# Gate weights kept in HBM tile by tile instead of column chunk by column chunk

## The reference

```
s = einsum('thpd,hpnd->thpn', q, sub_keys)              # 8 heads, 2 halves, 128 keys each
top_s, top_i = top_k(s, 16);  cand = sums of all pairs
best_s, best_c = top_k(cand, 16)                        # 16 experts per head and token
ids = i1 * 128 + i2;  gates = softmax(best_s)           # 128 experts per token
a = einsum('tkd,td->tk', expert_down[ids], x)
act = gelu(a) * gates
y = einsum('tk,tkd->td', act, expert_up[ids])
```

## Time and profile before

| | |
|---|---|
| median of 3 runs | 1579.66 us (1577.53 to 1579.83) |
| profiled execution | 1579.83 us, of which the span is 1578.0 us |
| mean granted TensorE clock | 0.987 of full speed |
| TensorE busy | 94% of the span |
| VectorE, ScalarE, GpSimd busy | 76%, 40%, 37% |
| HBM read, written | 360.49 MB, 42.99 MB |

### The profile page before, as it was taken

One profiled execution on the slowest core, in us unless ns is written; L12 is line 12 of the kernel. 1 busy time (PEld: TensorE's weight loads), 2 busy tenths in 40 slices (PEclk: granted clock), 3 DMA queues, 4 the chain that ended last, 5 costly groups with the idle time before them and its releaser, 6 DMA issues.

```text
span 1578.0 us, 21497 instructions
## 1 busy us (share of the span) xinstructions
PE 1487.3 (94%) x7670; PEld 1279.7 (81%) x7670; DVE 1199.6 (76%) x2406; ACT 623.7 (40%) x984; POOL 583.8 (37%) x459
## 2 busy tenths in 40 slices
PE   3999997999999889999978999999999999999997
PEld 3575545998888779999977888888888888888886
DVE  6546435678999987888836788787787888888887
ACT  1114333343434446666633333333333333333333
POOL 0000011225455436898821333343333443444340
PEclk9999998999999999999989999999999999999999
DMA  9962300446544436678678998999999999999983
GB/s 332 358 236 107 107 27 14 137 154 215 172 160 150 132 117 215 236 288 288 245 281 309 346 358 323 358 342 339 355 308 367 334 342 368 356 332 370 349 310 124
DMA packets 167945, 404.89 MB, mean 257 GB/s; under 512 B 20824, under 2 KB 83872, under 8 KB 166816
## 3 DMA queue, kind: packets, MB, share of 16 engines
q1 hardware_dynamic: 129152, 243.87, 44.2%
q0 software_dynamic: 36864, 134.23, 23.8%
q10 hardware_dynamic: 1824, 25.43, 4.0%
HBM read 360.49 MB, written 42.99 MB: 256 GB/s over the span
## 4 chain that ended last, share of the span: by engine, by line
PE 62%; DVE 12%; issue 4%; POOL 2%; DMA 2%; ACT 2%; SPq 0%; DVEq 0%; POOLq 0%; ACTq 0%
PE bank L1703 11%; PE bank L1704 10%; PE bank L1705 10%; PE bank L1647 8%; PE bank L1649 8%; PE bank L1648 8%; PE bank L1685 4%; DVE dlo L1209 2%; DVE cand L1253 2%; POOL gated L678 2%; DMA down<-in_down_t 1%; DVE topi L1199 1%; DVE top L1196 1%; PE bank L1592 1%; PE bank L1591 1%
## 5 line engine op out<-in xcount | busy, mean ns | idle before, releaser
L1647 PE MATMUL bank<-h2hi,dhi 128*128 128x384 f32 x1024 | 351.4, 343 | 38.2 <-DVE dlo L1209 36.8
L1649 PE MATMUL bank<-h2hi,dlo 128*128 128x384 f32 x1024 | 346.0, 338 | 0.0
L1648 PE MATMUL bank<-h2lo,dhi 128*128 128x384 f32 x1024 | 345.8, 338 | 0.0
L1209 DVE TENSOR_TENSOR dlo<-down,dhi 128x1024 fp32r<-128x1024 f32 x128 | 168.0, 1313 | 179.5 <-ACT dhi L826 179.4
L1703 PE MATMUL bank<-uhi,ahi 128*128 128x512 f32 x768 | 300.1, 391 | 3.5 <-DVE ulo L1381 3.5
L1704 PE MATMUL bank<-ulo,ahi 128*128 128x512 f32 x768 | 300.0, 391 | 0.0
L1705 PE MATMUL bank<-uhi,alo 128*128 128x512 f32 x768 | 299.6, 390 | 0.0
L645 POOL DMA_INDIRECT rows<-in_peer_down,ids x128 | 156.0, 1219 | 259.6 <-DVE rows L1222 221.1
L645 POOL DMA_INDIRECT rows<-in_peer_up,ids x128 | 159.5, 1246 | 246.2 <-DVE y L1231 221.9
L1647 PEld LDWEIGHTS bank<-h2hi,dhi 128*128 128x128 f32 x1024 | 194.7, 190 | 47.2 <-DVE dlo L1209 43.0
L1648 PEld LDWEIGHTS bank<-h2lo,dhi 128*128 128x128 f32 x1024 | 195.0, 190 | 2.7
(11 more groups left out here) (198 smaller groups left out, 2019.7 us busy)
## 6 DMA issues: line engine op xcount, KB each, us to landing
down<-in_down_t SPq DMA_DIRECT2D x128, 512.0 KB, 5.5
up<-in_peer_up SPq DMA_DIRECT2D x128, 512.0 KB, 6.6
ada<-in_w_ada SPq DMA_DIRECT2D x12, 2048.0 KB, 16.3
gate<-gates_dram SPq DMA_DIRECT2D x32, 768.0 KB, 10.4
gates_dram<-stage ACTq DMA_DIRECT2D x5, 4096.0 KB, 13.6
gel_dram<-gel SPq DMA_DIRECT2D x80, 192.0 KB, 2.1
gelu<-gel_dram SPq DMA_DIRECT2D x80, 192.0 KB, 5.8
wq<-in_peer_query SPq DMA_DIRECT2D x16, 512.0 KB, 4.7
```

The lines of the kernel that those rows point to most:

```text
L1209: ve.tensor_tensor(dlo[s][:], down[s][:], dhi[s][:].bitcast(F32), ALU.subtract).then_inc(dve_dlo, 1)
L1647: pe.matmul(bank[7 * s][:, 0:TD], dhi[s][:, k, :], h2hi[:, k, 0:TD], start=k == 0, stop=False)
L1648: pe.matmul(bank[7 * s][:, 0:TD], dhi[s][:, k, :], h2lo[:, k, 0:TD], start=False, stop=False)
L1649: last = pe.matmul(bank[7 * s][:, 0:TD], dlo[s][:, k, :], h2hi[:, k, 0:TD], start=False, stop=k == KT - 1)
```

## The change

The HBM tensor that holds the gates between the two stretches gets another order of axes. Before it is `[chunk, p, tile, 64 tokens]`; after it is `[tile, p, 384 tokens]`. So:

- A store still moves the same bytes of the same `stage` buffer, 4 MB per full chunk. Before, a partition's 32 KB land in one piece. After, they land as 128 pieces of 64 tokens (256 bytes), one in each tile's block, and with all partitions that makes 16384 pieces per chunk.
- A load fetches one tile (192 KB, 1536 bytes per partition) instead of four (768 KB, in pieces of 1 KB). 128 loads replace 32, in three buffers `gate0` to `gate2` instead of two for each of two groups. Each load waits for the product that last read its buffer.
- VectorE's product reads its gates as one plain row of 384 instead of six pieces of 64.
- The freed room changes places: one of the two late `rows` buffers moves from the second `stage` buffer's room to the first one's, so that its first gather waits for fewer stores. SyncE's wait for the second part of the last store moves to the first up step that needs it, and the last early tile's steps are written in another order.

```diff
-        gate = [[r(f"gate{g}_0", [CHUNKS, GSET, CHUNK_T])] for g in range(2)]
+        gate = [r(f"gate{i}", [TD]) for i in range(SLOTS)]
+        gelu = [r(f"gelu{i}", [TD]) for i in range(SLOTS)]
+        rows += [r(f"rows{ROWS - 2}", [D])]
...
-        gates_dram = nc.dram_tensor("gates_dram", [CHUNKS, KEYS, TILES, CHUNK_T], F32).ap()
+        gates_dram = nc.dram_tensor("gates_dram", [TILES, KEYS, TD], F32).ap()
...
-            def load_gates(n):
-                g, k = int(n >= EARLY), n % EARLY // GSET
-                sp.dma_start(gate[g][k % 2][:], gates_dram[:, :, n:n + GSET, :].rearrange("w p i t -> p w i t")
-                             ).then_inc(gate_in[g][k % 2], 16)
+            def load_gate(u):
+                if u >= SLOTS:
+                    sp.wait_ge(dve_act, u - SLOTS + 1)
+                sp.dma_start(gate[u % SLOTS][:], one(gates_dram, UPS[u])).then_inc(gate_in[u % SLOTS], 16)
...
             early(EARLY - 2)
-            next_down(EARLY - 1, 1)
             sp.wait_ge(stored[1], 16 * (CHUNKS // 2 - 1))
             sp.wait_ge(stored_part[0], 32)
-            for n in (0, EARLY):
-                load_gates(n)
-            store_gel(EARLY - 1, 1)
+            for u in range(SLOTS):
+                load_gate(u)
+            early(EARLY - 1)
             next_down(EARLY, 0)
...
+                        sp.wait_ge(stored_part[1], 32)
                         for s in range(2):
                             sp.wait_ge(gel_out[s], 16 * (EARLY // 2))
+                    load_gate(u)
                     load_gel(u)
                     load_up(u)
-                    for first in range(0, TILES, GSET):
-                        if first % EARLY and max(UP_AT[first - 2], SLOTS) == u:
-                            sp.wait_ge(stored_part[1], 32)
-                            if first % EARLY >= 2 * GSET:
-                                sp.wait_ge(dve_act, UP_AT[first - GSET - 1] + 1)
-                            load_gates(first)
...
             for n in range(asked, ROW_OPS):
-                if n == DOTS_EARLY + ROWS_KEPT:
+                if n == DOTS_EARLY + ROWS_KEPT + ROWS_ROUNDS - 1:
...
             def store_chunk(w, keys_1, signal):
-                act.dma_start(gates_dram[w, :, keys_1, :], stage[w % 2][:, keys_1, :]).then_inc(signal, 16)
+                act.dma_start(gates_dram[keys_1, :, w * CHUNK_T:(w + 1) * CHUNK_T].rearrange("i p t -> p i t"),
+                              stage[w % 2][:, keys_1, :]).then_inc(signal, 16)
...
-                ve.tensor_tensor(gelu[j][:].rearrange("p (w t) -> p w t", w=CHUNKS),
-                                 got[:].rearrange("p (w t) -> p w t", w=CHUNKS),
-                                 gate[g][k % 2][:, :, UPS[u] % GSET, :], ALU.mult).then_inc(dve_act, 1)
+                ve.wait_ge(gate_in[j], 16 * (u // SLOTS + 1))
+                ve.tensor_tensor(gelu[j][:], got[:], gate[j][:], ALU.mult).then_inc(dve_act, 1)
```

More of the change, by code:

```diff
@@ L116 @@
 assert sorted(UPS) == list(range(TILES))
-GSET = 4
-assert EARLY % GSET == 0 and TILES % GSET == 0 and 2 * GSET <= 16
 AHEAD = 2
@@ L343, in build_block @@
         alo = [r(f"alo{i}", [TD], F32R) for i in range(SLOTS)]
-        gelu = [r(f"gelu{i}", [TD]) for i in range(2)]
         r = Region(nc, stage_at, stage_at + KEYS * CHUNK_T * 4)
@@ L347, in build_block @@
         ulo += [r(f"ulo{i}", [D], F32R) for i in range(1, SLOTS)]
-        gelu += [r("gelu2", [TD])]
-        gate = [[r(f"gate{g}_0", [CHUNKS, GSET, CHUNK_T])] for g in range(2)]
+        gate = [r(f"gate{i}", [TD]) for i in range(SLOTS)]
+        gelu = [r(f"gelu{i}", [TD]) for i in range(SLOTS)]
+        rows += [r(f"rows{ROWS - 2}", [D])]
         r = Region(nc, stage_at + KEYS * CHUNK_T * 4, stage_at + 2 * KEYS * CHUNK_T * 4)
-        for g in range(2):
-            gate[g].append(r(f"gate{g}_1", [CHUNKS, GSET, CHUNK_T]))
-        rows += [r(f"rows{i}", [D]) for i in range(ROWS_KEPT + ROWS_HEADS, ROWS)]
+        rows += [r(f"rows{ROWS - 1}", [D])]
         yn = [r(f"yn{i}", [D]) for i in range(2)]
@@ L391, in build_block @@
         up_in = [sem(f"up_in{i}") for i in range(SLOTS)]
-        gate_in = [[sem(f"gate_in{g}_{i}") for i in range(2)] for g in range(2)]
+        gate_in = [sem(f"gate_in{i}") for i in range(SLOTS)]
         gel_in = [sem(f"gel_in{i}") for i in range(SLOTS)]
@@ L554, in _ @@
             sp.wait_ge(stored[0], 16 * (CHUNKS // 2))
-            sp.wait_ge(act_g, TD // 4)
             for u in range(SLOTS):
@@ L558, in _, with in_part0 @@
             early(EARLY - 2)
-            next_down(EARLY - 1, 1)
             sp.wait_ge(stored[1], 16 * (CHUNKS // 2 - 1))
             sp.wait_ge(stored_part[0], 32)
-            for n in (0, EARLY):
-                load_gates(n)
-            store_gel(EARLY - 1, 1)
+            for u in range(SLOTS):
+                load_gate(u)
+            early(EARLY - 1)
             next_down(EARLY, 0)
-            assert all(n < AFTER_G or n >= EARLY for n in UPS[:SLOTS])
+            def in_part0(n):
+                return n < 16 or EARLY <= n < EARLY + 16
+            whole_u = next(u for u, n in enumerate(UPS) if not in_part0(n))
+            assert all(n < AFTER_G or n >= EARLY for n in UPS[:whole_u])
             u = SLOTS
@@ L573, in _ @@
                 elif u < TILES:
-                    if u == SLOTS:
+                    if u == whole_u:
+                        sp.wait_ge(stored_part[1], 32)
                         for s in range(2):
                             sp.wait_ge(gel_out[s], 16 * (EARLY // 2))
+                    load_gate(u)
                     load_gel(u)
                     load_up(u)
-                    for first in range(0, TILES, GSET):
-                        if first % EARLY and max(UP_AT[first - 2], SLOTS) == u:
-                            sp.wait_ge(stored_part[1], 32)
-                            if first % EARLY >= 2 * GSET:
-                                sp.wait_ge(dve_act, UP_AT[first - GSET - 1] + 1)
-                            load_gates(first)
                     u += 1
@@ L1369, in activations @@
                         ve.wait_ge(dve_alo, u - SLOTS + 1)
-                g, k = int(UPS[u] >= EARLY), UPS[u] % EARLY // GSET
-                ve.wait_ge(gate_in[g][k % 2], 16 * (k // 2 + 1))
-                ve.tensor_tensor(gelu[j][:].rearrange("p (w t) -> p w t", w=CHUNKS),
-                                 got[:].rearrange("p (w t) -> p w t", w=CHUNKS),
-                                 gate[g][k % 2][:, :, UPS[u] % GSET, :], ALU.mult).then_inc(dve_act, 1)
+                ve.wait_ge(gate_in[j], 16 * (u // SLOTS + 1))
+                ve.tensor_tensor(gelu[j][:], got[:], gate[j][:], ALU.mult).then_inc(dve_act, 1)
             def parts_lo(u):
```

## The result

The changed kernel takes 1589.13 us (median of seven runs, 1583.71 to 1594.43), the kernel before on the same occasion 1577.53 us (seven, 1576.98 to 1581.32). The ratio is 1.0054 with a 95% interval of 1.0034 to 1.0076: slower by half a per cent. Forecast were 1695 us in a range of 1605 to 1790. The profiled execution took 1590.72 us, 10.9 more than the profiled one of before.

The account below looks back on a forecast made before the run. TensorE was taken to bound the kernel, with store issues holding ScalarE and so stopping it. 107.5 + 6.7 + 4.1 - 2.7 = +115.6 us on 1579.8 gave 1695.4 us, range 1605 to 1790.

Parts of the forecast that it names:

- What bounds the kernel: Whole span: TensorE is busy for 94%; cheaper VectorE or DMA work in the plan stretch is worth nothing.
- A chunk has 1025: ScalarE stands for 875 of them: Store issues of full chunks: entries per engine beyond about 150 hold ScalarE 22.4 us; five chunks cost +107.5 us.
- The 150 entries of the prediction: DMA queue: about 150 entries per engine can wait, worked out from SyncE's long issues at the trace's start.
- A piece of 256 bytes: Gate stores: each small write takes 25.6 ns per engine, the length of one read record.
- Rival 1: Gate stores: each small write costs double, 37.6 ns, giving 1758 us; chance 0.20 for 1740 to 1800.
- From a hold to TensorE's delay: Gates stretch: a 26.6 us hold, less cover, plus slow clock, costs TensorE 21.5 us per full chunk.
- B - 7.4 + 2.3: Cost per full chunk: B is hold plus other traffic, 26.6 us; 7.4 is TensorE's cover, 2.3 the slow clock.
- The last chunk: Last store, four parts: ScalarE free after 24 us, TensorE going on at 825.1 against 818.36 before.
- +6.7, +4.1 and -2.7: Last chunk: TensorE goes on later, +6.7 us; one down tile further back, +4.1; smaller first gate load, -2.7.
- Rival 3: Stores: the issue doesn't hold ScalarE and down loads slip between small pieces; 1567 us, chance 0.10, of which 0.06 faster.
- the cheap end of the failed step: Store hold: the queue takes more or a piece is cheap; 1618 us at 11 ns, chance 0.12 for 1600 to 1640.
- the three signs given for being wrong: Store issues under 7 us; TensorE waiting in the plan for gates; stores landing long after ScalarE is free.

Follow-up runs that it names:

- the pairs: Changed kernel with each of five full chunks stored by two DMAs, of 127 tiles and 1 tile: 1659.5 us big first, 1585.95 us small first, one run each.
- big part last: Changed kernel with the last chunk's two last parts swapped, so 128, 128, 256, then 512 pieces per engine: 1586.84 us, ratio 1.0032.
- the third experiment: Changed kernel with each of five full chunks stored by two DMAs, a big one of 127 tiles, then a small one of 1 tile: 1659.5 us, one run.
- the pair in the other order: Changed kernel with each of five full chunks stored by two DMAs, first 1 tile, then 127: 1585.95 us, one run.
- the second experiment: Changed kernel with the load of down tile EARLY+1 put ahead of the first three gate loads, as in the kernel before: 1583.14 us, ratio 1.0020.
- both edits: Changed kernel with the last chunk stored by one DMA and the down load ahead of the gate loads: 1568.92 us, ratio 0.9930; again 1574.33 us, 0.9953.
- stores alone: New layout with the changed kernel's stores, but gates loaded four tiles at a time in SyncE's order of the kernel before: 1584.03 us, ratio 1.0021.
- before with 4 KB: Kernel before with only the HBM layout changed, so that stores have pieces of 4 KB: 1572.43 us, ratio 0.9957.
- loads alone: Kernel before, its layout and stores kept, with the changed kernel's loads of one tile, each 768 pieces of 256 bytes: 1581.88 us, ratio 1.0016.

## Why the prediction was wrong, step by step

**What bounds the kernel: right.** The plan stretch is TensorE's own, and nothing in the loads, the DMA engines or VectorE's product changed it: the rest is 729.6 to 732.4 us in all kernels. Even a DMA share of 1.00 did not.

**"A chunk has 1025: ScalarE stands for 875 of them": this step failed.** The term was 107.5 us and measured 0: five issues of 0.37 us. The long issues of SyncE in the earlier trace rows were read as a limit on the entries of *one* DMA. Each of them stood behind other big DMAs, and the rows hold no case of a DMA of very many pieces with nothing in front. The rule that fits all runs is that the pieces counted are those of the DMAs ahead, less some room. The traces' packet records give the room: whenever an issue that had stood returned, at a last chunk or at the pairs, the DMAs ahead of it still had 11 to 108 pieces per engine to start. The start of the kernel before has the same: 96 when the issue of 5.29 us ended, and 97 when the next one did at 28.01. The 150 entries of the prediction are those 96 and the DMA's own 64, and the own ones do not count. A chunk stored by one DMA has nothing ahead of it, since the chunks come 31 to 34 us apart and one lands in 28.8. That the earlier trace rows shows 0.34 us for a store told nothing either way, as that DMA had few pieces.

**A piece of 256 bytes: 25.6 ns taken, about 20 measured** (20.3 behind 1016 pieces; (2.62 + 4.86 + 10.12) / 768 = 22.9 in the last chunk of the kernel after; 26 with the big part last). The spacing of the reads, 18.8 ns, was the better end. The packet record of one such write lasts 18 ns (median at the first chunk of the third experiment). Rival 1, writes at double cost (37.6 ns), is refuted by both. The Trainium skill (DMA: Bandwidth & Descriptors, "Specifications") has the engine read, modify and write below 512 bytes. These runs show no doubled price for it: writes of 256 bytes come every 20.3 ns, reads every 18.8.

**From a hold to TensorE's delay: right.** B - 7.4 + 2.3 with the 20.7 us of the third experiment gives 15.6 per chunk and 78 for five; measured were 70 (medians) to 74 (against the pair in the other order). So this step was sound: with a hold at every chunk and the measured price of a piece the sum would have been near.

**The last chunk: right in mechanism, and in size by luck.** Here there were DMAs ahead, and ScalarE did stand: 18.1 us for a forecast of 24. The terms +6.7, +4.1 and -2.7 add up to +8.1, and the turnover grew by 8.4, but not by these terms:

- Counted from the issue of the last store, TensorE's long pause ended after 20.9 us, before after 20.1. That is +0.8 for the forecast +6.7, and the 5.9 us between them are those by which the hold was shorter.
- Behind the pause there are six down tiles up to the first up product where there were five (48 matmuls of L1639 against 40 of L1647): +4.2, as forecast.
- There is a second pause, of 1.9 us. The down load whose issue follows `gel` is out only at 819.5, and TensorE stops again until 830.2. The sum did not have it.
- The load of the first gates gave nothing back: the wait for `ulo` grew by 1.0 us where 2.7 were to go. The change also puts a down load behind the gate loads on SyncE, and I had costed the moves on that queue only in the plan. By the second experiment this place costs 1 us in the turnover and 1.6 in the slow clock behind it.

**The rest of the 10.6 us**, 2.2 before the last store, belongs to no step. Of these 0.9 lie before the first store, and 1.3 between the first and the last, where GpSimd's instruction took 1.24 us on average in the profiled execution of before and 1.35 in that of after. In a single execution this can't be told from nothing. The traces hold one thing more. Where GpSimd was fast (0.92 to 0.94 us), the way from the first store to the last took 155.1 us with small pieces (both edits, stores alone) and 157.1 and 158.3 with pieces of 4 KB and longer (before with 4 KB, loads alone). The new layout may thus gain 2 to 3 us in the gates stretch; no run was made to test it.

**Rival 3** (the issue doesn't hold, the down loads slip between small pieces) was given 1567 us and a chance of 0.10. It was right for five chunks of six. When the sixth is one DMA as well and the down load stands where it was, the time is 1568.92 us, and 1574.33 in the second run. The 8.3 us pause is then gone as this rival had it: the down load issued at 802.81 is in use at 809.10, 6.3 us later. What kept the change from being a gain was thus the division of the last chunk into four parts, which had been free with few pieces, and to a lesser degree the new place of the down load.

**The range** left this out, since its lower end was the cheap end of the failed step. Of the three signs given for being wrong the first came true, as the issues of full chunks stayed under 7 us, and so did the third: the stores land 28.8 us after an issue of 0.37.

## What to carry to other kernels

On a queue that a compute engine issues from, look at what stands *ahead* of each DMA. One of very many pieces was free to issue here, and the next one paid for it, at about 20 ns per piece and engine. So give a store of small pieces one DMA and let no other issue follow soon. If it must be in parts, put the part with the most pieces last (here the hold fell from 18.1 to 14.0 us by that; a gain in time is likely and not shown). Long pieces have the opposite fault: they hold up other loads that share the engines. A layout with pieces of 4 KB instead of 4 to 32 KB gained 0.4% by itself. And before a long issue in a trace is taken for a property of its DMA, ask what was queued before it.

## What was not expected of the hardware

- The issue of a DMA of 16384 pieces took 0.37 us, and of one with 1 piece per partition 0.34 us; an issue of 8 pieces per engine behind one of 1016 took 20.64 us. How much may stand ahead before an issue is held is settled only roughly: 48 pieces per engine did not hold it (four parts in pieces of 4 KB, 2.62 us), and held issues returned with 11 to 108 left.
- While a store in small pieces was under way on ScalarE's queue, SyncE's issues were longer too: three loads of 192 KB took 3.49 and 3.80 us to issue, and 1.31 and 1.33 without one. That the store is the cause is not shown.
- A load of 512 KB landed after 13.27 and 12.62 us beside stores mostly in pieces of 16 and 8 KB, and after 8.65 us beside the same bytes in pieces of 4 KB, in the same place of the same program.
- 4 MB in pieces of 256 bytes landed in 28 to 33 us among the other traffic, and in 21.8 us when ScalarE stood behind each of them (big then small).
- GpSimd's 128x128 tensor-scalar instruction took 0.94 us on average in one profiled execution of a kernel and 1.35 in another. With it the time from the first to the last store of the gates stretch went from 155.1 to 160.9 us. The cause is open.
